# Up projection of a gated FFN: both halves of the moving operand in one matmul, with the low sums copied out and added

## The chip, the cores and the metric

The kernel runs on one core of a Trainium2 chip. The metric is the device time of one execution in microseconds (us): the median of the runs. A core has five engines that run their own instruction streams and meet at semaphores: TensorE (PE in the profile; its weight loads are PEld), VectorE (DVE), ScalarE (ACT), GpSimd (POOL) and SyncE (SP), which here issues the transfers.

## The reference

A small network on 256 tokens of width 1024, batch 1, in float32. Five feed-forward blocks (FFNs) stand in it: four with a causal depthwise convolution of three taps (D_FF 2816), each behind a mixer, and one plain gated block at the end, behind a fifth mixer.

```python
def conv_gated_ffn(xn, w_up, conv_w, conv_b, w_down):
    h = causal_depthwise_conv(xn @ w_up, conv_w, conv_b)
    a, g = jnp.split(h, 2, axis=-1)
    return (jax.nn.silu(g) * a) @ w_down

def swiglu(h, w_gate, w_up, w_down):
    return (jax.nn.silu(h @ w_gate) * (h @ w_up)) @ w_down
```

The mixers (two attentions, a spatial gating, a state space layer, and the last one with a context operand) are untouched.

## The kernel before

**Precision by splitting.** Every large product is made of three: operand and weight are each split into a high part (the value as float32r) and the low rest (what is left of it); `product` (lines 1683, 1684, 1685) adds high x high, weight high x operand low, and weight low x operand high into the same PSUM columns. The operand stands feature-major in XH (highs) and XL (lows), 8 tiles of 128 features by up to 512 columns; the FFNs use the first 256 columns, one per token.

**The weight stream.** Weights come in units of 128 x 2048 floats (1 MB), in the order in which they are used, into a ring of three (raw). For each unit ScalarE copies out the high part (`split_hi`, line 381, writes whi) and VectorE subtracts for the low part (`split_lo`, line 896, writes wlo). whi and wlo are rings of three too: ScalarE waits until TensorE is done with the unit three before (semaphore w_used), and TensorE waits for w_lo before it starts a unit. So the splits run at most three units ahead.

**An FFN** has 33 units: 22 up units (one per tile of 128 value features and 128 gate features) and 11 down units (one per two up units). An up unit j is 2 halves (m) x 8 feature tiles x 3 products of 256 columns = 48 products; its sums, 2 x 256 columns, fill one PSUM bank, 4 or 5 by turns. A down unit has 48 products as well and adds into banks 0 to 3, which hold the whole output and are zeroed ahead with a matmul of zeros. TensorE's order is up 0, up 1, then in a loop (up, up, down) ten times, then the last down. TensorE waits for pp_taken of unit j-2 before it writes a bank again.

**After an up unit** of a conv FFN, VectorE's `take` (line 1068) reads the bank, multiplies it with the row of token scales RSTD, and writes UA in SBUF; ScalarE makes the middle tap and bias of both halves (line 486, waits for pp_taken), VectorE adds two taps each (line 1082, four instructions), ScalarE applies silu to the gate half (line 489), VectorE multiplies (line 1089, writes HID). After two such units ScalarE copies the high part of the hidden pair into HH (line 502) and VectorE subtracts for HL (line 1102), the down unit's operand. HH has one buffer: it waits for the down unit before. In the plain FFN there is no take: silu (line 492) and the multiply (line 1096) read the bank.

**The order is written out by hand**, one program per engine, each strictly in order. A loop iteration (nine in a conv FFN on ScalarE and VectorE, with a head and a tail around them) is, for both up units: ScalarE `split_hi`, taps, silu; VectorE take, `split_lo`, taps, multiply; then a third `split_hi` and HH, a third `split_lo` and HL. The split that stands in the iteration belongs to a later unit: the first to the down unit, the other two to the next two up units.

**Scales.** The first two up units of a conv FFN run while the token scales are still being made; `scale_sums` puts small matmuls among their products, and their results into bank 6. In the fourth FFN the operand of the context is made between iterations (`context_high`, line 411, and `context_operand`, line 1035, called every second iteration as `aside`). In the second FFN GpSimd computes tables for the state space layer beside it.

Of the kernel before, what the change touches and what calls it, by code (L numbers as in the profile page):

```python
# [23 lines left out]
P = 128  # L24
# [102 lines left out]
def program(nc, wst, mst, crow, vec, cst, xin, sgw, sgb, sbc, ctxin, ropes, out):  # L127
    with ExitStack() as ctx:
# [9 lines left out]
        XH = sb("XH", [P, KT, 2 * T], R32)  # L138
        XL = sb("XL", [P, KT, 2 * T], R32)
# [40 lines left out]
        SQ = ar(2048, KT, T)  # L180

# [45 lines left out]
        def s5(i):  # L227
# [58 lines left out]
                 "c_in", "c_row", "ctx_rms", "ctx_inv", "ctx_diag", "ctx_row", "ml_in0", "ml_in1", "ml_used",  # L286
# [84 lines left out]
        def _(act):  # L371
# [67 lines left out]
            def scales():  # L439
# [3 lines left out]
                act.activation(RMSC, PS[:, 6, 0:2], ACT.Sqrt, bias=vcol("eps", 0), scale=1.0 / D)\  # L443
# [29 lines left out]
            def ffn(layer, conv=True, aside=None, tail=None, then=None):  # L473
                u0, q0, up0, hid0 = t.u, t.pp, t.up, t.hid

                def up(j, it=None):
# [3 lines left out]
                    if conv:  # L480
                        act.wait_ge(S["pp_taken"], q0 + j + 1 + 2 * k)
# [8 lines left out]
                    else:  # L490
                        act.wait_ge(S["w_used"], u + 1 + 3 * k)
                        act.activation(SG[:, j % 2, :], PS[:, 4 + (q0 + j) % 2, T:2 * T], ACT.Silu)\
                            .then_inc(S["silu_ready"], 1)

                def hidden(h, it=None):
                    k = 0 if it is None else it

                    act.wait_ge(S["hid_ready"] if conv else S["pp_taken"], (up0 if conv else q0) + 2 * h + 2 + 2 * k)
                    if h > 0:

                        act.wait_ge(S["w_used"], u0 + 2 + 3 * h + 3 * k)
                    act.activation(HH[:, :, :], HID, ACT.Copy).then_inc(S["hh_ready"], 1)

                if conv:
                    scales()
# [382 lines left out]
        def _(dve):  # L888
# [54 lines left out]
            def scales():  # L943
# [12 lines left out]
                dve.tensor_copy(RSTD, PS[:, 6, T:2 * T]).then_inc(S["rstd_row"], 1)  # L956
# [71 lines left out]
            def context_operand(p):  # L1028

                if p == 0:  # L1030
                    dve.wait_ge(S["ctx_in"], 32)
                    dve.wait_ge(S["ctx_row"], 1)
                    link(dve.tensor_copy(RSTX, PS[:, 6, 0:T]))
# [26 lines left out]
            def ffn(layer, conv=True, aside=None, then=None):  # L1060
                u0, q0, up0, hid0 = t.u, t.pp, t.up, t.hid

                def take(j, it=None):
                    k = 0 if it is None else it
                    u = u0 + 2 + 3 * (j // 2 - 1) + j % 2 if j >= 2 else u0 + j
                    bank = PS[:, 4 + (q0 + j) % 2, :].rearrange("p (a b) -> p a b", a=2)
                    dve.wait_ge(S["w_used"], u + 1 + 3 * k)
                    dve.tensor_tensor(UA[:, j % 2], bank, RSTD.unsqueeze(1).broadcast_to([P, 2, T]), ALU.mult)\  # L1068
                        .then_inc(S["pp_taken"], 1)

                def up(j, it=None):
                    k = 0 if it is None else it
                    bank = PS[:, 4 + (q0 + j) % 2, :].rearrange("p (a b) -> p a b", a=2)
                    if conv:

                        dve.wait_ge(S["conv0"], up0 + j + 1 + 2 * k)
                        for back in (1, 2):
# [10 lines left out]
                        dve.wait_ge(S["silu_ready"], up0 + j + 1 + 2 * k)  # L1088
                        dve.tensor_tensor(HID[:, j % 2, :], CA[:, j % 2, 0, :], SG[:, j % 2, :], ALU.mult)\
                            .then_inc(S["hid_ready"], 1)  # L1090
                    else:
                        if j >= 2 and j % 2 == 0:

                            dve.wait_ge(S["hl_ready"], hid0 + j // 2 + k)
                        dve.wait_ge(S["silu_ready"], up0 + j + 1 + 2 * k)
                        dve.tensor_tensor(HID[:, j % 2, :], bank[:, 0, :], SG[:, j % 2, :], ALU.mult)\
                            .then_inc(S["pp_taken"], 1)
# [7 lines left out]
                if conv:  # L1105
                    scales()
                for j in range(2):
                    if conv:
                        take(j)
# [5 lines left out]
                for p, (b, e) in enumerate(parts(n - 1, aside)):  # L1115
                    if aside:
                        aside(p)
                    with dve.Fori(0, e - b) as it:
                        for j in range(2):
                            if conv:  # L1120
                                take(2 + 2 * b + j, it)
# [6 lines left out]
                for j in range(2):  # L1128
                    if conv:
                        take(2 * n + j)  # L1130
# [546 lines left out]
        def _(pe):  # L1677
# [75 lines left out]
            def scale_sums(unit, m, k):  # L1753

                if (unit, m, k) == (0, 1, 3):
                    pe.wait_ge(S["square_sum"], t.free + 1)
                    for c in range(2):
                        for i in range(2):
                            mm = pe.matmul(PS[:, 6, c:c + 1], SQ[:, i, c * P:(c + 1) * P], ones[:, 0:1],
# [757 lines left out]
```

## Time and profile before

| | |
|---|---|
| median of 3 runs | 1827.54 us (1827.36 to 1828.07) |
| the profiled execution, its time | 1829.06 us |
| its span, first to last instruction | 1827.2 us |
| TensorE matmuls busy | 1708.1 us, 93% |
| TensorE weight loads busy (beside the matmuls) | 1616.3 us, 88% |
| VectorE busy | 1248.8 us, 68% |
| ScalarE busy | 844.6 us, 46% |
| GpSimd busy | 163.0 us, 9% |
| mean granted TensorE clock | 0.976 of full |

The profile is of one execution. Busy shares are averages over stages with different limits. A matmul's recorded duration includes its way through the array, so two in a row overlap in the records; what paces TensorE is the distance from start to start. Idle time is put down to the semaphore event that came last.

### The profile page before, as it was taken

How to read it: one execution, taken by the hardware profiler on the slowest of the kernel's cores; microseconds unless marked ns; L12 is line 12 of the kernel's file. 1: busy time of each engine (PE TensorE's matmuls, PEld its weight loads, DVE VectorE, ACT ScalarE, POOL GpSimd, SP SyncE). 2: the span in 40 equal slices, each digit the busy share in tenths (PEclk: the TensorE clock that was granted, in tenths of full speed). 3: DMA queues.
4: the chain of work that ended last, by engine and by line, in shares of the span. 5: the costliest groups of instructions: out<-in, count | busy, mean ns of one | idle time of the engine just before them, and what ended most of it. 6: DMA issues, size and time to landing. Idle time of an engine off the chain costs nothing.

```text
span 1827.2 us, 34733 instructions
## 1 busy us (share of the span) xinstructions
PE 1708.1 (93%) x14503; PEld 1616.3 (88%) x14514; DVE 1248.8 (68%) x1580; ACT 844.6 (46%) x962; POOL 163.0 (9%) x130
## 2 busy tenths in 40 slices
PE   6999999889899997799999999999979899999997
PEld 6979999889899985699999988999978579889997
DVE  5847777786877759767777774777774575664444
ACT  5355554546455530355545445555554533143333
POOL 1002000104910062200000101000000000000000
PEclk9999999999999999999999999999989999899999
DMA  7904545544455423444555761454432121035551
GB/s 299 333 1 162 190 178 184 184 162 152 150 181 184 164 91 117 163 162 162 182 184 181 270 252 47 179 191 168 183 111 93 69 93 70 24 138 184 184 184 69
DMA packets 40050, 286.50 MB, mean 157 GB/s; under 512 B 4576, under 2 KB 4576, under 8 KB 5664
## 3 DMA queue, kind: packets, MB, share of 16 engines
q1 hardware_dynamic: 39024, 280.99, 42.8%
q10 hardware_dynamic: 944, 4.33, 0.7%
q8 instruction: 63, 1.03, 0.2%
q14 instruction: 19, 0.16, 0.0%
HBM read 284.25 MB, written 1.05 MB: 156 GB/s over the span
## 4 chain that ended last, share of the span: by engine, by line
PE 64%; DVE 17%; ACT 9%; issue 6%; POOL 2%; DMA 1%; DVEq 0%; ACTq 0%; POOLq 0%; SPq 0%
PE PS L1683 19%; PE PS L1684 18%; PE PS L1685 18%; ACT whi L381 4%; DVE wlo L896 4%; DVE AR L1082 4%; ACT AR L486 1%; POOL AR L2389 1%; PE PS L1779 1%; DVE AR L1193 1%; DVE XL L940 1%; DVE AR L1190 1%; ACT AR L576 1%; ACT AR L578 1%; PE PS L2235 1%
## 5 line engine op out<-in xcount | busy, mean ns | idle before, releaser
L1683 PE MATMUL PS<-XH,whi 128*128 128x256 f32 (+1 forms) x2696 | 788.8, 293 | 45.0 <-DVE wlo L896 23.8
L1684 PE MATMUL PS<-XL,whi 128*128 128x256 f32 (+1 forms) x2696 | 780.2, 289 | 0.0
L1685 PE MATMUL PS<-XH,wlo 128*128 128x256 f32 (+1 forms) x2696 | 780.1, 289 | 0.0
L896 DVE TENSOR_TENSOR wlo<-raw,whi 128x2048 fp32r<-128x2048 f32 x240 | 558.9, 2331 | 187.7 <-ACT whi L381 187.6
L1683 PEld LDWEIGHTS PS<-XH,whi 128*128 128x128 f32 x2696 | 523.6, 194 | 58.1 <-issue 34.0
L1684 PEld LDWEIGHTS PS<-XL,whi 128*128 128x128 f32 x2696 | 524.1, 194 | 4.4 <-issue 0.2
L1685 PEld LDWEIGHTS PS<-XH,wlo 128*128 128x128 f32 x2696 | 523.7, 194 | 4.1
L381 ACT ACTIVATE whi<-raw 128x2048 fp32r<-128x2048 f32 x240 | 456.0, 1902 | 72.8 <-PE PS L1685 48.4
L1683 PE MATMUL PS<-HH,whi 128*128 128x256 f32 x880 | 251.8, 286 | 13.0 <-DVE HL L1102 8.5
L1685 PE MATMUL PS<-HH,wlo 128*128 128x256 f32 x880 | 251.0, 285 | 0.0
L1684 PE MATMUL PS<-HL,whi 128*128 128x256 f32 x880 | 250.8, 285 | 0.0
L1683 PEld LDWEIGHTS PS<-HH,whi 128*128 128x128 f32 x880 | 170.7, 194 | 14.8 <-DVE HL L1102 9.5
L1082 DVE SCALAR_TENSOR_TENSOR AR<-AR,VEC 128x255 f32<-128x255 f32 (+1 forms) x352 | 161.7, 501 | 15.4 <-ACT AR L486 4.7
L1684 PEld LDWEIGHTS PS<-HL,whi 128*128 128x128 f32 x880 | 170.6, 194 | 0.0
L1685 PEld LDWEIGHTS PS<-HH,wlo 128*128 128x128 f32 x880 | 170.5, 194 | 0.0
L489 ACT ACTIVATE AR<-AR 128x256 f32<-128x256 f32 x88 | 36.7, 418 | 268.4 <-DVE AR L1082 268.4
L2389 POOL TENSOR_TENSOR AR<-AR 128x512 f32<-128x512 f32 x24 | 56.0, 2335 | 916.3 <-ACT AR L435 916.2
L486 ACT ACTIVATE AR<-AR,VEC 128x256 f32<-128x256 f32 x176 | 95.6, 590 | 86.1 <-DVE AR L1068 86.1
L1068 DVE TENSOR_TENSOR AR<-PS,SM 128x512 f32<-128x512 f32 x88 | 60.7, 689 | 27.2 <-PE PS L1685 24.1
L1683 PE MATMUL PS<-whi,XH 128*128 128x256 f32 x256 | 74.1, 289 | 2.5 <-DVE XL L940 2.5
L1684 PE MATMUL PS<-wlo,XH 128*128 128x256 f32 x256 | 73.3, 286 | 0.0
L1685 PE MATMUL PS<-whi,XL 128*128 128x256 f32 x256 | 73.2, 286 | 0.0
(336 smaller groups left out, 1583.7 us busy)
## 6 DMA issues: line engine op xcount, KB each, us to landing
raw<-wst SPq DMA_DIRECT2D x248, 1024.0 KB, 4.8
AR<-mst SPq DMA_DIRECT2D x17, 1024.0 KB, 6.2
XT<-x_in SPq DMA_DIRECT2D x2, 512.0 KB, 6.0
AR<-crow ACTq DMA_DIRECT2D x2, 512.0 KB, 5.8
AR<-sbc ACTq DMA_DIRECT2D x1, 1024.0 KB, 6.6
AR<-ctxin ACTq DMA_DIRECT2D x1, 1024.0 KB, 5.8
y_out<-XT SPq DMA_DIRECT2D x1, 1024.0 KB, 3.9
AR<-sgw ACTq DMA_DIRECT2D x1, 512.0 KB, 3.7
```

The lines of the kernel that those rows point to most:

```text
L381: act.activation(whi[:, r, :], raw[:, u % RING, :], ACT.Copy).then_inc(S["w_hi"], 1)
L486: a = act.activation(CA[:, j % 2, i, :], UA[:, j % 2, i, :], ACT.Identity, bias=cb, scale=w2)
L489: act.activation(SG[:, j % 2, :], CA[:, j % 2, 1, :], ACT.Silu).then_inc(S["silu_ready"], 1)
L576: act.activation(EX[:, p % 2, :], ZC[:, p % 2, :], ACT.Exp).then_inc(S["ex_ready"], 1)
L578: act.activation(LN[:, p % 2, :], EX[:, p % 2, :], ACT.Ln, bias=1.0)\
L896: dve.tensor_tensor(wlo[:, r, :], raw[:, u % RING, :], whi[:, r, :].bitcast(F32), ALU.subtract)\
L1068: dve.tensor_tensor(UA[:, j % 2], bank, RSTD.unsqueeze(1).broadcast_to([P, 2, T]), ALU.mult)\
L1082: ins = dve.scalar_tensor_tensor(y, UA[:, j % 2, i, 0:T - back], w, y, ALU.mult, ALU.add)
L1683: pe.matmul(dst, sh, mh, start=first, stop=False, **kw)
L1684: pe.matmul(dst, sh, ml, start=False, stop=False, **kw)
L1685: return pe.matmul(dst, sl, mh, start=False, stop=last, **kw)
L2389: ins = pool.tensor_tensor(SQ[:, 0:2, :], SQ[:, 0:2, :], SQ[:, 2 * mp:2 * mp + 2, :], ALU.add)
```

## The change

Only the up units of the FFNs change.

TensorE: XH and XL become two views of one tensor XX, so that for a feature tile the 256 highs and the 256 lows of the operand can be read as one moving operand of 512 columns. A group of three products becomes two: weight high x (highs, lows), 512 columns, into a whole bank; and weight low x highs, 256 columns, into the bank's first half. The two halves m take two banks, so unit j takes the pair 4, 5 or the pair 6, 7 by turns. The bank's second half then holds the sums over the lows, which must be added to the first.

ScalarE: a new `lows(j)`, in the program just ahead of the taps of unit j (behind the high split of that half iteration), waits for the unit's products and copies the second halves of both banks (512 columns in all) to LS in SBUF. VectorE: `take` waits for that copy and adds PSUM's first halves and LS into UA; in conv FFNs a second instruction multiplies UA with RSTD. In the plain FFN silu and the multiply read UA instead of the bank.

Banks 6 and 7 being in use, the scale sums of an FFN go to bank 3, and the zeroing of bank 3 moves behind up 1 and waits for their readers.

```diff
-        XH = sb("XH", [P, KT, 2 * T], R32)
-        XL = sb("XL", [P, KT, 2 * T], R32)
+        XX = sb("XX", [P, KT, 4 * T], R32)
+        XH, XL = XX[:, :, 0:2 * T], XX[:, :, 2 * T:4 * T]
...
+        LS = ar(2048, 2, 2, T)
...
+                def lows(j, u, k):
+
+                    b = 4 + 2 * ((q0 + j) % 2)
+                    act.wait_ge(S["w_used"], u + 1 + 3 * k)
+                    act.activation(LS[:, j % 2], PS[:, b:b + 2, T:2 * T], ACT.Copy).then_inc(S["lo_out"], 1)
+
                 def up(j, it=None):
...
                     if conv:
+                        lows(j, u, k)
                         act.wait_ge(S["pp_taken"], q0 + j + 1 + 2 * k)
...
-                        act.wait_ge(S["w_used"], u + 1 + 3 * k)
-                        act.activation(SG[:, j % 2, :], PS[:, 4 + (q0 + j) % 2, T:2 * T], ACT.Silu)\
-                            .then_inc(S["silu_ready"], 1)
+                        lows(j, u, k)
+                        act.wait_ge(S["pp_taken"], q0 + j + 1 + 2 * k)
+                        act.activation(SG[:, j % 2, :], UA[:, j % 2, 1, :], ACT.Silu).then_inc(S["silu_ready"], 1)
...
-                    bank = PS[:, 4 + (q0 + j) % 2, :].rearrange("p (a b) -> p a b", a=2)
-                    dve.wait_ge(S["w_used"], u + 1 + 3 * k)
-                    dve.tensor_tensor(UA[:, j % 2], bank, RSTD.unsqueeze(1).broadcast_to([P, 2, T]), ALU.mult)\
-                        .then_inc(S["pp_taken"], 1)
+                    b = 4 + 2 * ((q0 + j) % 2)
+                    dve.wait_ge(S["lo_out"], up0 + j + 1 + 2 * k)
+                    ins = dve.tensor_tensor(UA[:, j % 2], PS[:, b:b + 2, 0:T], LS[:, j % 2], ALU.add)
+                    if conv:
+                        ins.then_inc(S["up_sum"], 1)
+                        dve.wait_ge(S["up_sum"], up0 + j + 1 + 2 * k)
+                        ins = dve.tensor_tensor(UA[:, j % 2], UA[:, j % 2], RSTD.unsqueeze(1).broadcast_to([P, 2, T]), ALU.mult)
+                    ins.then_inc(S["pp_taken"], 1)
...
-                            mm = product(PS[:, 4 + (q0 + j) % 2, m * T:(m + 1) * T],
-                                         w(slot, kt * 256 + m * P, kt * 256 + m * P + P),
-                                         x(kt), kt == 0, kt == KT - 1)
+                            high, low = w(slot, kt * 256 + m * P, kt * 256 + m * P + P)
+                            both = XX[:, kt, :].rearrange("p (h s t) -> p h s t", h=2, s=2)[:, :, 0, :]
+                            pe.matmul(PS[:, b + m, :].rearrange("p (h t) -> p h t", h=2), high, both, start=(kt == 0), stop=False)
+                            mm = pe.matmul(PS[:, b + m, 0:T], low, XH[:, kt, 0:T], start=False, stop=(kt == KT - 1))
...
-                for b in range(4):
+                def zero(b):
                     pe.matmul(PS[:, b, :], ZB[:, 0:P], ZB[:, :], start=True, stop=False, skip_group_check=True)
+                for b in range(3):
+                    zero(b)
                 up(0)
                 up(1)
+                if free:
+                    pe.wait_ge(S["rstd_row"], t.free)
+                    if t.free == 8:
+                        pe.wait_ge(S["ctx_taken"], 1)
+                zero(3)
```

ScalarE, from the start of a loop iteration of the first FFN to the second high split in it, before (AR are UA, the taps' sums and silu's result by turns; REGISTER_ALU and ISA rows compute loop addresses):

```order
L380 ISA [waits w_loaded2]
L381 ACTIVATE whi<-raw 128x2048 [waits w_used]
L481 ISA
L486 ISA [waits pp_taken]
L486 ACTIVATE AR<-AR,VEC 128x256
L486 ISA
L486 ACTIVATE AR<-AR,VEC 128x256
L488 REGISTER_ALU
L489 ACTIVATE AR<-AR 128x256 [waits conv2]
L378 REGISTER_ALU
L380 REGISTER_ALU [waits w_loaded0]
L381 ACTIVATE whi<-raw 128x2048 [waits w_used]
```

and after:

```order
L382 ACTIVATE whi<-raw 128x2048 [waits w_used]
L480 REGISTER_ALU
L481 ACTIVATE AR<-PS 128x512 [waits w_used]
L489 ISA
L494 ISA [waits pp_taken]
L494 ACTIVATE AR<-AR,VEC 128x256
L494 ISA
L494 ACTIVATE AR<-AR,VEC 128x256
L496 REGISTER_ALU
L497 ACTIVATE AR<-AR 128x256 [waits conv2]
L379 REGISTER_ALU
L382 ACTIVATE whi<-raw 128x2048 [waits w_used,w_loaded0]
```

The copy L481, which waits for the unit's products, now stands between the high split and the taps; the taps' wait is behind it.

VectorE, the same iteration, from the multiply that makes the first HID to the second low split, before:

```order
L1089 TENSOR_TENSOR AR<-AR 128x256 [waits silu_ready]
L1067 REGISTER_ALU
L1068 TENSOR_TENSOR AR<-PS,SM 128x512 [waits w_used]
L895 REGISTER_ALU
L896 TENSOR_TENSOR wlo<-raw,whi 128x2048 [waits w_hi]
```

and after:

```order
L1104 TENSOR_TENSOR AR<-AR 128x256 [waits silu_ready]
L1076 REGISTER_ALU
L1077 TENSOR_TENSOR AR<-PS,AR 128x512 [waits lo_out]
L1081 TENSOR_TENSOR AR<-AR,SM 128x512 [waits up_sum]
L903 REGISTER_ALU
L904 TENSOR_TENSOR wlo<-raw,whi 128x2048 [waits w_hi]
```

The take L1068 has become the add L1077, which waits for ScalarE's copy, and the multiply L1081, which waits for the add; the low split stands behind both.

TensorE, the start of its loop of the first FFN, before:

```order
L1797 ISA [waits pp_taken]
L1683 MATMUL PS<-XH,whi 128x256 [waits w_lo]
L1684 MATMUL PS<-XL,whi 128x256
L1685 MATMUL PS<-XH,wlo 128x256
L1683 MATMUL PS<-XH,whi 128x256
L1684 MATMUL PS<-XL,whi 128x256
L1685 MATMUL PS<-XH,wlo 128x256
```

and after:

```order
L1801 ISA [waits pp_taken]
L1809 MATMUL PS<-XX,whi 128x512 [waits w_lo]
L1810 MATMUL PS<-XX,wlo 128x256
L1809 MATMUL PS<-XX,whi 128x512
L1810 MATMUL PS<-XX,wlo 128x256
L1809 MATMUL PS<-XX,whi 128x512
L1810 MATMUL PS<-XX,wlo 128x256
```

Three products of 256 columns have become one of 512 and one of 256, and the unit's waits are those of before.

## Rows read from the trace of the kernel before

**Rows 1.** Timeline, VectorE, first FFN, HL alone: start, us, engine, line
```profile
171.30 0.69 DVE L1102 TENSOR_TENSOR HL<-AR,HH 128x512 fp32r<-128x512 f32 x1 [0.70 <-ACT HH L502]
...
238.68 0.69 DVE L1102 TENSOR_TENSOR HL<-AR,HH 128x512 fp32r<-128x512 f32 x1
...
255.95 0.69 DVE L1102 TENSOR_TENSOR HL<-AR,HH 128x512 fp32r<-128x512 f32 x1
...
339.25 0.69 DVE L1102 TENSOR_TENSOR HL<-AR,HH 128x512 fp32r<-128x512 f32 x1 [0.69 <-ACT HH L502]
```

**Rows 2.** Timeline, VectorE, first FFN, second loop iteration
```profile
188.09 0.69 DVE L1102 TENSOR_TENSOR HL<-AR,HH 128x512 fp32r<-128x512 f32 x1
188.69 0.69 DVE L1068 TENSOR_TENSOR AR<-PS,SM 128x512 f32<-128x512 f32 x1
189.29 2.28 DVE L896 TENSOR_TENSOR wlo<-raw,whi 128x2048 fp32r<-128x2048 f32 x1
191.49 1.90 DVE L1082 SCALAR_TENSOR_TENSOR AR<-AR,VEC 128x255 f32<-128x255 f32 x4
193.88 0.42 DVE L1089 TENSOR_TENSOR AR<-AR 128x256 f32<-128x256 f32 x1 [0.48 <-ACT AR L489]
...
195.68 2.29 DVE L896 TENSOR_TENSOR wlo<-raw,whi 128x2048 fp32r<-128x2048 f32 x1 [0.70 <-ACT whi L381]
...
204.28 0.68 DVE L1102 TENSOR_TENSOR HL<-AR,HH 128x512 fp32r<-128x512 f32 x1
```

**Rows 3.** Timeline, ScalarE, the same iteration
```profile
193.42 0.42 ACT L489 ACTIVATE AR<-AR 128x256 f32<-128x256 f32 x1 [2.77 <-DVE AR L1082]
193.75 1.90 ACT L381 ACTIVATE whi<-raw 128x2048 fp32r<-128x2048 f32 x1
...
200.14 1.90 ACT L381 ACTIVATE whi<-raw 128x2048 fp32r<-128x2048 f32 x1
201.94 0.61 ACT L502 ACTIVATE HH<-AR 128x512 fp32r<-128x512 f32 x1
202.46 1.90 ACT L381 ACTIVATE whi<-raw 128x2048 fp32r<-128x2048 f32 x1
```

**Rows 4.** Timeline, VectorE, first and last HL, second and fourth FFN
```profile
456.78 1.90 DVE L1102 TENSOR_TENSOR HL<-AR,HH 128x512 fp32r<-128x512 f32 x1 [0.70 <-ACT HH L502]
...
633.38 0.69 DVE L1102 TENSOR_TENSOR HL<-AR,HH 128x512 fp32r<-128x512 f32 x1 [0.69 <-ACT HH L502]
...
1164.83 0.69 DVE L1102 TENSOR_TENSOR HL<-AR,HH 128x512 fp32r<-128x512 f32 x1 [0.70 <-ACT HH L502]
...
1336.92 0.69 DVE L1102 TENSOR_TENSOR HL<-AR,HH 128x512 fp32r<-128x512 f32 x1 [0.69 <-ACT HH L502]
```

**Rows 5.** Timeline, TensorE, last mixer, 512-column products
```profile
1370.52 0.39 PE L1683 MATMUL PS<-XH,whi 128*128 128x512 f32 x1
...
1371.20 0.39 PE L1683 MATMUL PS<-XH,whi 128*128 128x512 f32 x1
```

**Rows 6.** Groups by line and shape: count, busy us, mean ns, idle before
```profile
L719 ACT ACTIVATE AR<-PS 128x512 f32<-128x512 f32 x8 | 4.3, 596 | 21.4 <-PE PS L1685 21.4
```

**Rows 7.** Timeline, VectorE then ScalarE, fourth FFN, between two iterations
```profile
1200.40 0.69 DVE L1102 TENSOR_TENSOR HL<-AR,HH 128x512 fp32r<-128x512 f32 x1
...
1201.52 0.91 ACT L411 ACTIVATE XH<-AR,MODV 128x256 fp32r<-128x256 f32 x2 [2.84 <-DVE AR L1035]
1202.33 1.90 ACT L381 ACTIVATE whi<-raw 128x2048 fp32r<-128x2048 f32 x1
```

**Rows 8.** Timeline, TensorE, two waits (in brackets the wait, its releaser)
```profile
340.00 0.39 PE L1683 MATMUL PS<-HH,whi 128*128 128x256 f32 x1 [1.75 <-DVE HL L1102]
...
495.93 0.54 PE L1683 MATMUL PS<-XH,whi 128*128 128x256 f32 x1 [3.36 <-DVE wlo L896]
```

**Rows 9.** Windows behind these waits: stretch, us, PE busy, PEclk, DMA
```profile
340.10:343.50 3.40, 3.40 (x29) 1.00 0.04 14
496.00:499.40 3.40, 3.40 (x16) 0.50 0.63 219
```

More of the change, by code:

```diff
@@ L490, in up @@
                     else:
[L491 to L493 removed]
+                        lows(j, u, k)
+                        act.wait_ge(S["pp_taken"], q0 + j + 1 + 2 * k)
+                        act.activation(SG[:, j % 2, :], UA[:, j % 2, 1, :], ACT.Silu).then_inc(S["silu_ready"], 1)
                 def hidden(h, it=None):
                     k = 0 if it is None else it
[L498 removed]
+                    act.wait_ge(S["hid_ready"], up0 + 2 * h + 2 + 2 * k)
                     if h > 0:
@@ L504, in ffn @@
                 if conv:
-                    scales()
+                    scales(3)
                 act.preload_act_table(ACT.Silu)
@@ L1087, in up @@
                                 ins.then_inc(S["conv2"], 1)
[L1088 to L1097, printed above, removed]
+                    if j >= 2 and j % 2 == 0 and not conv:
+                        dve.wait_ge(S["hl_ready"], hid0 + j // 2 + k)
+                    dve.wait_ge(S["silu_ready"], up0 + j + 1 + 2 * k)
+                    value = CA[:, j % 2, 0, :] if conv else UA[:, j % 2, 0, :]
+                    dve.tensor_tensor(HID[:, j % 2, :], value, SG[:, j % 2, :], ALU.mult).then_inc(S["hid_ready"], 1)
                 def hidden(h, it=None):
@@ L1105, in ffn @@
                 if conv:
-                    scales()
+                    scales(3)
                 for j in range(2):
-                    if conv:
-                        take(j)
+                    take(j)
                     ahead(u0 + j)
@@ L1119, in ffn @@
                         for j in range(2):
-                            if conv:
-                                take(2 + 2 * b + j, it)
+                            take(2 + 2 * b + j, it)
                             split_lo(s1 + 3 * b + j, it)
@@ L1128, in ffn @@
                 for j in range(2):
-                    if conv:
-                        take(2 * n + j)
+                    take(2 * n + j)
                     split_lo(s1 + j)
@@ L1751, in tokens, with scale_sums @@
                 t.u += 1
-            def scale_sums(unit, m, k):
+            def scale_sums(unit, m, k, bank=6):
                 if (unit, m, k) == (0, 1, 3):
@@ L1771, in scale_sums @@
                     for c in range(2):
-                        mm = pe.matmul(PS[:, 6, c * P:(c + 1) * P], ones, DG[:, c * P:(c + 1) * P], start=True, stop=True)
+                        mm = pe.matmul(PS[:, bank, c * P:(c + 1) * P], ones, DG[:, c * P:(c + 1) * P], start=True, stop=True)
                     mm.then_inc(S["ctx_row"], 1)
```

21 lines of the change are left out of this document (11 added, 10 removed).

## The prediction

> **What bounds the kernel now.** Read the by-engine part of the page first: TensorE is busy nearly all the time, so the question is what paces it in the five feed-forward blocks (FFNs), the only part that changes. The start times of one VectorE instruction that occurs once per loop iteration, the subtraction that makes HL, answer it. In the first FFN's steady part two of them stand 17.27 us apart [rows 1], and an iteration holds 3 weight units of 48 products: 17.28 / 144 = 0.120 us a product. TensorE is the bound, at its own pace.
>
> Then the timeline of VectorE and ScalarE in an iteration where TensorE happened to be ahead. There HL follows HL after 204.28 - 188.09 = 16.19 us [rows 2], with no wait for TensorE in it. These two engines pass work to each other in program order, and the chain closes on itself. Read from start to start: HL to take 0.60; take to split 0.60; split to taps 2.20; taps to silu 1.93; silu to the next high split 0.33; that to its low split 1.93; split to taps 2.20; taps to silu 1.93; silu to high split 0.33; to low split 1.93; to HL 2.21 [rows 2, 3]. The sum is 16.19. So this loop is only 1.1 us shorter than TensorE's 17.28; that is all the slack there is, and shares of busy time do not show it.
>
> The same instruction in the second and the fourth FFN (first to last of 11) spans 176.60 and 172.09 us, against 339.25 - 171.30 = 167.95 in the first (the third repeats the first) [rows 1, 4]. In these two the VectorE loop already bounds part of the time: GpSimd work stretches VectorE instructions in the second, and preparation of the context operand stands between iterations in the fourth.
>
> **The change, part by part.**
>
> *TensorE.* A group of three products of 256 columns costs 0.360 us. It becomes one of 512 and one of 256. The trace has 512-column products of the same operands in the last mixer: three take 0.68 us, 0.227 each [rows 5]. A group becomes 0.227 + 0.120 = 0.347, 0.013 less; a unit of 16 groups 0.213 less; an iteration with two up units 16.85 us instead of 17.28. If TensorE bounded everywhere, 110 up units would give 23.4 us. The Trainium skill (TensorE: Matmul & The Clock Gate, Back-to-back issue gap) gives a spacing of N/2.4 + 2.5 ns; by it a group would fall from 328 to 325 ns, which would leave only some 4 us of the 23.4. The rows are above that formula by 11 ns at either width, so a fixed cost is paid per product, and I use the rows.
>
> *The copy (ScalarE).* A Copy of 128x512 out of two banks takes 0.596 us [rows 6], with a hand-over of 0.04 (silu 193.42 + 0.42 to the multiply at 193.88 [rows 2, 3]) 0.64. In each half of an iteration it stands behind a high split, 1.80 after that split's start (201.94 - 200.14); what follows HH starts 0.52 after it [rows 3].
>
> *The add and the multiply (VectorE).* Before, one instruction of 0.69 out of PSUM, the take, with 0.60 to the next [rows 2]. Now an add of the same shape, a hand-over to itself (0.69 + 0.04 = 0.73), and the multiply, which I price as the same instruction.
>
> *What this does to the loop.* Odd unit: before, its low split began 0.33 + 1.93 = 2.26 us after the even unit's silu, with take long done. Now ScalarE must finish the high split before it copies: 0.33 + 1.80 + 0.64 (copy) + 0.73 (add) + 0.60 (multiply) = 4.10. That is 1.84 more. Even unit: HL start to low split was 1.20; now ScalarE runs HH, a high split and the copy (from HL's predecessor 1.80 + 0.52 + 1.80 + 0.64 = 4.76 after a high split's start, against 4.14 for HL), so the add begins 0.62 after HL, then 0.73 + 0.60: 1.95, 0.75 more. The loop becomes 16.19 + 1.84 + 0.75 = 18.78 us. TensorE at 16.85 now waits 1.9 us in every iteration.
>
> *A conv FFN.* Up to the first HL: 0.73 + 1.84 = 2.6 later. First iteration: HH to the copy's end is 0.52 + 1.80 + 0.64, less 0.65 to HL (HH's 0.61 and a hand-over), so the add comes 2.31 after HL instead of 0.62: 18.78 + 1.69 = 20.47. Eight at 18.78: 150.24. Last (no third split, so HL follows silu by 0.46 + 0.47 + 0.65 instead of 4.47): 15.89. Together 186.6 against 167.95, +18.6; with the start +21.2. First and third FFN: 42.4.
> Second: 176.60 before. The stretching by GpSimd (8.65 over the first FFN visible, more than that hidden by slack) adds about 10 in full: 196.6, so +20.0 + 2.6 = 22.6.
> Fourth: at each of four places the context operand puts two VectorE and two ScalarE steps ahead of the next high split. From HL to the end of the two ScalarE steps is 1202.33 - 1200.40 = 1.93, and HL to the add becomes 1.93 + 1.80 + 0.64 = 4.37 [rows 7] instead of 0.62, 3.75 more, three times; the first time 2.5 (it replaces 2.31, and has a copy of 0.46 more); the fifth about 0.8. 186.6 + 14.6 = 201.2 against 172.09: +29.1 + 2.6 = 31.7.
> The last FFN has no taps and no multiply; its engines have room, so it keeps TensorE's pace: 22 x 0.213 = -4.7. Its end is set by HH waiting for the product unit ahead, which does not change.
> Sum: 42.4 + 22.6 + 31.7 - 4.7 = +92.0.
>
> *The clock.* TensorE now waits longer, most of all ahead of each conv FFN's last down unit: HL starts 15.89 after the one before, while TensorE is done after 0.11 + 5.55 + 5.76 = 11.4, so with HL's own 0.7 it idles 5.2 us, where it idled 1.75 [rows 8]. After a wait of 1.75 the granted clock stayed 1.00 (2.4 GHz); after one of 3.36 it was 0.50 (1.2 GHz) for 3.4 us [rows 8, 9], which costs 1.7. Four times 1.7 is 6.8, on the path. The GpSimd stretch gets two more such waits, about 1.2 net. Elsewhere in the loop waits are about 1 us each. I add 8.
>
> Total: +100. The profiled execution took 1829.06 us (span 1827.2); 1929, or 1927.5 from the median of 1827.54. I say 1927.
>
> **The bounds.** Copy: from nothing on the path (then the two adds alone remain, 1.46 a loop, 17.65; the whole sum some 31 lower) to 0.73; I take the Copy row, the same form. Add and multiply: from 0.60 to 0.80 each. Cheap ends of both together lower the sum by some 20, dear ends raise it by 14; the clock from 0 to 16. Hence 1903 to 1949.
>
> **The rivals.**
> *TensorE stays the bound.* Then -23.4: 1829.1 - 23.4 = 1806, the other side. It needs the ScalarE-VectorE loop to stay below 16.85, thus to grow by less than 0.66 instead of 2.59. For it: both engines are busy only 68% and 46%. Against it: the 16.19 with nothing waiting for TensorE. Even with the copy free the two extra adds exceed 0.66. 4%.
> *The copy hides.* If sums end early enough and ScalarE slips the copy into a wait, only the adds lengthen the loop: 17.65, total +61 + 8: about 1897. Against it: ScalarE's order puts a 1.9 us split right ahead of each odd copy. 8%.
> *The clock falls in every iteration.* With 1.9 us of wait in 18.8, in two pieces of 0.8 and 1.0, a fall of 3.4 us per iteration would cost 1.7, of which 0.54 is slack before an even copy: 36 x 1.16 = 42 more, 1969. For it: a fall follows every long wait. Against: 1.75 in one piece brought none [rows 8, 9]. 7%.
> *The edit does nothing measurable*, gain and loss cancelling: the loop would have to be 17.3 to 17.4. 1%.
> The forecast itself has 80%.
>
> **How the numbers follow.** 1927 is the likeliest case; its own range, 1903 to 1949, holds nearly all of its 80%, so it is the range. No change can be told within 0.2%, about 3.7 us; the copy-hides and clock cases are slower too, so faster 4%, same 1%, slower 95%.
>
> **What will show it.** HL to HL in the first FFN near 18.8 us, not 16.9. Idle time ahead of the add should be put down to ScalarE's copy, and TensorE's idle time to the low split, twice an iteration. The product of 512 columns should be spaced 0.227 and the pair 0.347, visible in the last FFN, where HL stands 16.85 apart. Clock 0.50 at each conv FFN's end. Wrong would be: a copy much longer than 0.6, a pair slower than 0.36 (which in the conv FFNs would still be hidden), or a loop other than 18.8.

## The result

The changed kernel takes 1927.78 us (median of 4 runs, 1924.5 to 1932.19) against 1827.45 for the one before: the ratio is 1.0551, 95% interval 1.0535 to 1.0568. It is slower by 100 us; forecast were 1927, a range of 1903 to 1949, and 95% for slower.

The page of the changed kernel's profiled execution: the span, busy time by engine, and three groups of section 5 (count, busy us, mean ns, then idle time before and what ended it).

```profile
span 1923.6 us, 31472 instructions
## 1 busy us (share of the span) xinstructions
PE 1726.9 (90%) x12754; PEld 1533.7 (80%) x12754; DVE 1315.7 (68%) x1690; ACT 907.3 (47%) x1072; POOL 160.5 (8%) x130
...
L1809 PE MATMUL PS<-XX,whi 128*128 128x512 f32 x1760 | 640.9, 406 | 57.3 <-DVE wlo L904 53.9
L904 DVE TENSOR_TENSOR wlo<-raw,whi 128x2048 fp32r<-128x2048 f32 x240 | 559.0, 2332 | 115.1 <-ACT whi L382 115.0
...
L1077 DVE TENSOR_TENSOR AR<-PS,AR 128x512 f32<-128x512 f32 x110 | 75.8, 689 | 176.2 <-ACT AR L481 176.1
```

VectorE's add now idles 176.2 us ahead, 176.1 of it ended by ScalarE's copy (L481); before, the take idled 27.2 us, mostly for TensorE. And TensorE's wide products (L1809) idle 57.3 us ahead, 53.9 of it ended by the low split (L904). The span grew by 1923.6 - 1827.2 = 96.4 us.

The same instruction as in [rows 1], HL on VectorE, first FFN of the changed kernel (start, duration, line):

```profile
174.50 0.69 DVE L1109 TENSOR_TENSOR HL<-AR,HH 128x512 fp32r<-128x512 f32 x1 [0.70 <-ACT HH L510]
...
194.92 0.69 DVE L1109 TENSOR_TENSOR HL<-AR,HH 128x512 fp32r<-128x512 f32 x1
...
213.65 0.68 DVE L1109 TENSOR_TENSOR HL<-AR,HH 128x512 fp32r<-128x512 f32 x1
...
344.72 0.68 DVE L1109 TENSOR_TENSOR HL<-AR,HH 128x512 fp32r<-128x512 f32 x1
...
360.33 0.69 DVE L1109 TENSOR_TENSOR HL<-AR,HH 128x512 fp32r<-128x512 f32 x1 [0.70 <-ACT HH L510]
```

The iterations are 18.7 us long (213.65 - 194.92 = 18.73), where they were 16.2 to 17.3; the first is 20.42 and the last 15.61. The forecast was 18.78, 20.47 and 15.89. From the first HL to the last it is 185.83 us against 167.95 [rows 1].

One iteration of it, VectorE, the counterpart of [rows 2]:

```profile
232.37 0.69 DVE L1109 TENSOR_TENSOR HL<-AR,HH 128x512 fp32r<-128x512 f32 x1
232.97 0.68 DVE L1077 TENSOR_TENSOR AR<-PS,AR 128x512 f32<-128x512 f32 x1
233.69 0.69 DVE L1081 TENSOR_TENSOR AR<-AR,SM 128x512 f32<-128x512 f32 x1
234.30 2.29 DVE L904 TENSOR_TENSOR wlo<-raw,whi 128x2048 fp32r<-128x2048 f32 x1
236.50 1.89 DVE L1094 SCALAR_TENSOR_TENSOR AR<-AR,VEC 128x255 f32<-128x255 f32 x4
238.88 0.43 DVE L1104 TENSOR_TENSOR AR<-AR 128x256 f32<-128x256 f32 x1 [0.48 <-ACT AR L497]
241.17 0.69 DVE L1077 TENSOR_TENSOR AR<-PS,AR 128x512 f32<-128x512 f32 x1 [1.86 <-ACT AR L481]
241.89 0.69 DVE L1081 TENSOR_TENSOR AR<-AR,SM 128x512 f32<-128x512 f32 x1
242.50 2.28 DVE L904 TENSOR_TENSOR wlo<-raw,whi 128x2048 fp32r<-128x2048 f32 x1
...
251.09 0.68 DVE L1109 TENSOR_TENSOR HL<-AR,HH 128x512 fp32r<-128x512 f32 x1
```

And ScalarE, the counterpart of [rows 3]:

```profile
238.43 0.42 ACT L497 ACTIVATE AR<-AR 128x256 f32<-128x256 f32 x1 [2.77 <-DVE AR L1094]
238.75 1.90 ACT L382 ACTIVATE whi<-raw 128x2048 fp32r<-128x2048 f32 x1
240.56 0.58 ACT L481 ACTIVATE AR<-PS 128x512 f32<-128x512 f32 x1
...
248.76 0.61 ACT L510 ACTIVATE HH<-AR 128x512 fp32r<-128x512 f32 x1
249.28 1.90 ACT L382 ACTIVATE whi<-raw 128x2048 fp32r<-128x2048 f32 x1
251.08 0.57 ACT L481 ACTIVATE AR<-PS 128x512 f32<-128x512 f32 x1
```

VectorE ends the even unit's multiply at 238.88 + 0.43 and stands until 241.17. Meanwhile ScalarE, behind silu, runs the 1.9 us high split from 238.75, then the copy (240.56), and only the copy's end at 241.14 lets the add go. Silu 238.43 to low split 242.50 is 4.07 us (forecast 4.10, before 2.26). At the end of the iteration HL at 251.09 is followed by the add after 0.60 and the low split 1.33 after that (234.30 - 232.97): 1.93 in all, forecast 1.95.

The five FFNs, from first to last HL, in us; the rows of before are [rows 1, 4]:

| FFN | before | after | grew | forecast of the growth |
|---|---|---|---|---|
| first | 167.95 | 185.83 | 17.9 | 18.6 |
| second (GpSimd beside it) | 176.60 | 196.26 | 19.7 | 20.0 |
| third | 167.95 | 185.85 | 17.9 | 18.6 |
| fourth (context operand) | 172.09 | 204.75 | 32.7 | 29.1 |
| plain | 171.98 | 166.84 | -5.1 | -4.7 with its start |

What is left, 13.4 us, lies between the blocks: each block's first HL comes 2.3 to 3.2 us later after what precedes it. For the four conv FFNs these sum to 10.65 us, for the plain one it is 2.8.

The plain FFN's row must not be read as its gain. Its first and last HL, before and then after:

```profile
1635.19 0.69 DVE L1102 TENSOR_TENSOR HL<-AR,HH 128x512 fp32r<-128x512 f32 x1 [0.70 <-ACT HH L502]
...
1807.17 0.69 DVE L1102 TENSOR_TENSOR HL<-AR,HH 128x512 fp32r<-128x512 f32 x1 [5.64 <-ACT HH L502]
```

```profile
1736.72 0.69 DVE L1109 TENSOR_TENSOR HL<-AR,HH 128x512 fp32r<-128x512 f32 x1 [0.70 <-ACT HH L510]
...
1903.56 0.69 DVE L1109 TENSOR_TENSOR HL<-AR,HH 128x512 fp32r<-128x512 f32 x1 [2.61 <-ACT HH L510]
```

The first HL comes later and the iteration behind it is shorter by about as much (13.19 us against 16.40), so most of the -5.1 only makes up for the late start. From the fourth FFN's last HL to the plain one's last it is 470.25 us before (1807.17 - 1336.92) and 467.89 after (1903.56 - 1435.67): 2.4 less, half of the forecast 4.7, which counted the start too.

**One wait that was not forecast.** HL of the fourth FFN of the changed kernel, first, second and last:

```profile
1230.92 0.69 DVE L1109 TENSOR_TENSOR HL<-AR,HH 128x512 fp32r<-128x512 f32 x1 [0.69 <-ACT HH L510]
...
1258.43 0.69 DVE L1109 TENSOR_TENSOR HL<-AR,HH 128x512 fp32r<-128x512 f32 x1
...
1435.67 0.69 DVE L1109 TENSOR_TENSOR HL<-AR,HH 128x512 fp32r<-128x512 f32 x1 [0.70 <-ACT HH L510]
```

The first iteration is 27.51 us, not 20.47 + 2.5 = 23.0. TensorE's timeline says why (its second row is the wait ahead of the first FFN's last down unit, the counterpart of [rows 8]):

```profile
1232.09 0.58 PE L1837 MATMUL PS<-ZB 128*128 128x512 bf16 x1 [11.50 <-DVE AR L1041]
...
361.08 0.38 PE L1687 MATMUL PS<-HH,whi 128*128 128x256 f32 x1 [4.55 <-DVE HL L1109]
```

The zeroing of bank 3 waited 11.50 us for L1041, VectorE's copy of the context's scale row out of bank 3, which in program order stands behind the first HL.

**The clock.** TensorE's granted clock in two stretches of the changed kernel (us, PE busy, PEclk, DMA share, GB/s), behind the 4.55 us wait at 361.08 and at the place where the next stage starts:

```profile
361.40:364.80 3.40, 3.40 (x19) 0.52 0.02 7
377.20:380.60 3.40, 3.40 (x30) 1.00 0.93 320
```

and in the kernel before, at the start of that next stage:

```profile
356.10:359.50 3.40, 3.40 (x17) 0.50 0.89 320
```

The fall behind the last down unit's wait came as forecast, 0.52 for 3.4 us. But the kernel before has one of its own some 16 us later, which the changed kernel has not: here the fall moved, it was not added. The other three FFN ends are not all alike. Behind the second FFN it moved as well. Behind the third both stand in the changed kernel (0.55 from 1061.60, and again 0.55 from 1078). Behind the fourth the kernel before already has one, after a wait of the same 1.75 us as in [rows 8] (TensorE's row, then the window behind it):

```profile
1337.66 0.39 PE L1683 MATMUL PS<-HH,whi 128*128 128x256 f32 x1 [1.75 <-DVE HL L1102]
...
1338.60:1342.00 3.40, 3.40 (x20) 0.57 0.00 0
```

So of the four falls that were forecast there, one was new. And within the loop there is none: from the second HL of the changed kernel's first FFN to the tenth (194.92 to 344.72) the granted clock is 1.00.

### The profile page after: what moved, and what is told of

Read it like the earlier page. It is cut to its first block, busy times and chain, and to the rows that moved or that the text cites. A ratio compares the mean times of both kernels' runs of the same rounds, so it can differ in the third digit from the quotient of the medians.

```text
span 1923.6 us, 31472 instructions
## 1 busy us (share of the span) xinstructions
PE 1726.9 (90%) x12754; PEld 1533.7 (80%) x12754; DVE 1315.7 (68%) x1690; ACT 907.3 (47%) x1072; POOL 160.5 (8%) x130
## 4 chain that ended last, share of the span: by engine, by line
PE 40%; DVE 29%; ACT 14%; issue 13%; POOL 2%; DVEq 1%; DMA 1%; ACTq 0%; POOLq 0%; SPq 0%
ACT whi L382 9%; DVE wlo L904 8%; PE PS L1687 8%; PE PS L1688 8%; PE PS L1689 8%; DVE AR L1094 7%; PE PS L1809 5%; DVE AR L1077 3%; PE PS L1810 3%; DVE HL L1109 1%; ACT AR L481 1%; DVE AR L1081 1%; POOL AR L2402 1%; PE PS L1783 1%; DVE AR L1197 1%
## 5 line engine op out<-in xcount | busy, mean ns | idle before, releaser
L1809 PE MATMUL PS<-XX,whi 128*128 128x512 f32 x1760 | 640.9, 406 | 57.3 <-DVE wlo L904 53.9
L904 DVE TENSOR_TENSOR wlo<-raw,whi 128x2048 fp32r<-128x2048 f32 x240 | 559.0, 2332 | 115.1 <-ACT whi L382 115.0
L1810 PE MATMUL PS<-XX,wlo 128*128 128x256 f32 x1760 | 495.8, 282 | 0.0
L1809 PEld LDWEIGHTS PS<-XX,whi 128*128 128x128 f32 x1760 | 333.1, 189 | 156.4 <-DVE wlo L904 73.7
L1810 PEld LDWEIGHTS PS<-XX,wlo 128*128 128x128 f32 x1760 | 335.4, 191 | 0.2
L1687 PE MATMUL PS<-XX,whi 128*128 128x256 f32 (+1 forms) x936 | 283.3, 303 | 29.7 <-DVE wlo L904 15.4
L1687 PE MATMUL PS<-HH,whi 128*128 128x256 f32 x880 | 257.9, 293 | 38.2 <-DVE HL L1109 19.8
L1688 PE MATMUL PS<-XX,whi 128*128 128x256 f32 (+1 forms) x936 | 278.7, 298 | 0.0
L1689 PE MATMUL PS<-XX,wlo 128*128 128x256 f32 (+1 forms) x936 | 278.5, 297 | 0.0
L1687 PEld LDWEIGHTS PS<-XX,whi 128*128 128x128 f32 x936 | 183.3, 196 | 37.9 <-issue 30.7
L1077 DVE TENSOR_TENSOR AR<-PS,AR 128x512 f32<-128x512 f32 x110 | 75.8, 689 | 176.2 <-ACT AR L481 176.1
L1688 PEld LDWEIGHTS PS<-XX,whi 128*128 128x128 f32 x936 | 183.3, 196 | 4.4 <-issue 0.2
L1689 PEld LDWEIGHTS PS<-XX,wlo 128*128 128x128 f32 x936 | 182.9, 195 | 4.2
L1688 PEld LDWEIGHTS PS<-HL,whi 128*128 128x128 f32 x880 | 176.1, 200 | 0.0
L1689 PEld LDWEIGHTS PS<-HH,wlo 128*128 128x128 f32 x880 | 176.0, 200 | 0.0
L494 ACT ACTIVATE AR<-AR,VEC 128x256 f32<-128x256 f32 x176 | 96.4, 595 | 149.7 <-DVE AR L1081 149.7
```

Source lines behind the costliest of these rows:

```text
L494: a = act.activation(CA[:, j % 2, i, :], UA[:, j % 2, i, :], ACT.Identity, bias=cb, scale=w2)
L904: dve.tensor_tensor(wlo[:, r, :], raw[:, u % RING, :], whi[:, r, :].bitcast(F32), ALU.subtract)\
L1077: ins = dve.tensor_tensor(UA[:, j % 2], PS[:, b:b + 2, 0:T], LS[:, j % 2], ALU.add)
L1687: pe.matmul(dst, sh, mh, start=first, stop=False, **kw)
L1688: pe.matmul(dst, sh, ml, start=False, stop=False, **kw)
L1689: return pe.matmul(dst, sl, mh, start=False, stop=last, **kw)
```

## The experiments

The theory is the prediction's: ScalarE and VectorE form a closed loop in each conv iteration (taps, silu, splits, take), the copy and the add lengthen it by 1.84 + 0.75 us, and it overtakes TensorE. Its rival: the time comes from TensorE itself, from how the wide and narrow products run, or from its clock behind longer waits. Every ratio is to the kernel before, on the same chip. Differences from the changed kernel's 1927.78 us may be between chips, on which the kernel before took 1827.45 to 1828.08 us.

**products_only.** The changed products without the copy and the add; the sums over the operand's lows are left out. In the plain FFN, where VectorE had the add, it copies the first halves out instead.

```diff
-                        lows(j, u, k)
-                    dve.wait_ge(S["lo_out"], up0 + j + 1 + 2 * k)
-                    ins = dve.tensor_tensor(UA[:, j % 2], PS[:, b:b + 2, 0:T], LS[:, j % 2], ALU.add)
+                    dve.wait_ge(S["w_used"], u + 1 + 3 * k)
+                    ins = dve.tensor_tensor(UA[:, j % 2], PS[:, b:b + 2, 0:T], ..., ALU.mult)
```

> The changed products with neither the copy nor the add: VectorE's take multiplies the banks' first halves with the scales right away, as before the change. Left out of the computation: the sums over the operand's lows. Theory 1 (the ScalarE-VectorE chain bounds the changed kernel): that chain is back at 16.2 us an iteration, TensorE bounds again, now at 16.85, so HL to HL is 16.85 and the time falls below that of before, to about 1813 (conv FFNs -10, plain FFN -5). Theory 2 (the 512-column product itself, or its two-piece operand, is slow in the FFNs): HL to HL stays well above 17.28 and the time stays near the changed kernel's 1928. Theory 3 (the clock): falls of the granted clock remain without long waits.

1825.77 us, ratio 0.9987 (0.9978 to 0.9997). The loops are back under TensorE, so copy and add are what slowed the changed kernel; the rival, by which TensorE itself did, is out. But HL to HL is 17.07, not 16.85, and the bank 3 wait is there too (8.97 us of TensorE, first iteration of the fourth FFN 25.4 us against 19.32): two misses that together leave 2 us of the expected 15. The wait alone takes back 6.1; at 17.07 the products save 0.21 us an iteration where 0.43 was reckoned, half as much.

**three_products.** The changed kernel with three products a group. The sums over the highs and over the lows of the operand are interleaved in one bank, which changes what is summed; only its time is read.

```diff
-                            pe.matmul(PS[:, b + m, :]..., high, both, start=(kt == 0), stop=False)
+                            pe.matmul(PS[:, b + m, 0:T], high, XH[:, kt, 0:T], start=(kt == 0), stop=False)
+                            pe.matmul(PS[:, b + m, T:2 * T], high, XL[:, kt, 0:T], start=(kt == 0), stop=(kt == KT - 1), ...)
```

> The changed kernel with its copy, add and banks, but TensorE's group is three products of 256 columns again (weight high x highs into the first half, weight high x lows into the second, weight low x highs into the first). Theory 1: in the conv FFNs nothing changes, HL to HL stays at 18.73, since TensorE's 17.28 still fits; in the plain FFN it goes from 16.85 to 17.28, so about +5: 1932. Theory 2: without the 512-column product the time falls to near 1828.

1928.28 us, ratio 1.0552 (1.0535 to 1.057): the changed kernel's, where 1932 was expected. HL to HL stays 18.73 in the conv FFNs and goes from 17.07 to 17.28 in the plain one (first to last 169.19 against 166.84, so 2.4 us and not 5). In the conv FFNs the whole TensorE part of the change is invisible.

**no_mult.** The changed kernel without the multiply by the scales in the conv FFNs, which is left out of the computation.

```diff
-                    if conv:
-                        ins.then_inc(S["up_sum"], 1)
-                        dve.wait_ge(S["up_sum"], up0 + j + 1 + 2 * k)
-                        ins = dve.tensor_tensor(UA[:, j % 2], UA[:, j % 2], ..., ALU.mult)
```

> The changed kernel without the second VectorE instruction of the take in the conv FFNs. Left out of the computation: the scaling of the up sums by the token scales. Theory 1: the multiply is in the chain twice an iteration at about 0.73 each, so HL to HL goes from 18.73 to about 17.3 and the time falls by about 60, to 1866. Rival (only ScalarE's copy and what it waits for set the pace, VectorE's second instruction hides behind ScalarE): HL to HL stays within 0.3 of 18.7 and the time within 10 of 1928.

1862.56 us, ratio 1.02 (1.0183 to 1.0217), 65 less. Two HLs of its first FFN:

```profile
226.08 0.68 DVE L1105 TENSOR_TENSOR HL<-AR,HH 128x512 fp32r<-128x512 f32 x1
...
243.35 0.68 DVE L1105 TENSOR_TENSOR HL<-AR,HH 128x512 fp32r<-128x512 f32 x1
```

17.27 apart: the multiply was twice in the chain, at 0.73.

**copy_first.** The changed kernel with the copy ahead of the high split (`copied` is the wait and copy that stood in `up`).

```diff
                         for j in range(2):
+                            copied(2 + 2 * b + j, it)
                             split_hi(s1 + 3 * b + j, it)
-                            up(2 + 2 * b + j, it)
+                            up(2 + 2 * b + j, it)
```

> The changed kernel with one thing moved in the conv FFNs: ScalarE's copy of the low sums stands ahead of the high split of its half iteration, not behind it. Theory 1 (1.84 of the chain's growth in the odd unit is the copy waiting behind the split): the low split now begins 2.8 us after silu instead of 4.1, HL to HL falls from 18.73 to about 17.5 and the time by about 62, to 1866. Rival (the copy waits for TensorE, not for the split): less than 10 of it.

1869.19 us, ratio 1.0231 (1.0214 to 1.0248), 59 less. VectorE in its first FFN:

```profile
250.36 0.43 DVE L1115 TENSOR_TENSOR AR<-AR 128x256 f32<-128x256 f32 x1 [0.48 <-ACT AR L501]
250.84 0.69 DVE L1088 TENSOR_TENSOR AR<-PS,AR 128x512 f32<-128x512 f32 x1
251.57 0.69 DVE L1092 TENSOR_TENSOR AR<-AR,SM 128x512 f32<-128x512 f32 x1
252.65 2.29 DVE L915 TENSOR_TENSOR wlo<-raw,whi 128x2048 fp32r<-128x2048 f32 x1 [0.38 <-ACT whi L382]
```

The low split starts 2.74 us after silu (249.91), no longer 4.07. The last row shows one thing more: add and multiply are over at 252.26 (251.57 + 0.69), and the low split then waits 0.38 us for the high split. With the copy out of its way, the second VectorE instruction costs the odd unit nothing. The mean of HL to HL is about 17.7, a little above 17.5, since ScalarE now waits for TensorE before its split in the even unit.

**ctx_early.** The changed kernel with the context row copied earlier.

```diff
                     up(j)
+                    if aside and j == 0:
+                        dve.wait_ge(S["ctx_row"], 1)
+                        dve.tensor_copy(RSTX, PS[:, 3, 0:T]).then_inc(S["ctx_taken"], 1)
```

> The changed kernel, with the copy of the context's scale row out of bank 3 moved on VectorE from behind the first HL of the fourth FFN to behind its first up unit. Theory 1a (the zeroing of bank 3 waits for this copy and holds up TensorE by 11.5 us, which makes the first iteration 27.5 us instead of the forecast 22.9): the wait goes, the first iteration comes to about 23 and the total falls by 4 to 6, to 1923. Rival (TensorE's wait there is covered by the chain of the other two engines anyway): no change within 1 us.

1920.16 us, ratio 1.0508 (1.049 to 1.0525), 7.6 less by the medians and 6.2 in the profiled spans, a little more than the expected 4 to 6. The first iteration of the fourth FFN is 22.47 (27.51 - 22.47 = 5.0) and TensorE's wait at the zeroing 2.02 instead of 11.50.

**base_mid.** The kernel before with the high splits of the conv FFNs between taps and silu (`between` calls `split_hi`). HH now stands ahead of the third split.

```diff
                         a.then_inc(S["conv0"], 1)
+                        between()
                         act.wait_ge(S["conv2"], up0 + j + 1 + 2 * k)
...
-                            split_hi(s1 + 3 * b + j, it)
-                            up(2 + 2 * b + j, it)
-                        split_hi(s1 + 3 * b + 2, it)
-                        hidden(1 + b, it)
+                            up(2 + 2 * b + j, it, lambda: split_hi(s1 + 3 * b + j, it))
+                        hidden(1 + b, it)
+                        split_hi(s1 + 3 * b + 2, it)
```

> The kernel before the change, with one thing moved in the conv FFNs: ScalarE's high splits stand between the taps and silu of a unit (where it waits for VectorE's taps anyway), one split earlier than before. Theory 1 (a closed chain of the two engines, with the split behind silu in it) says that both 1.93 us pieces from split to split leave the chain, so it drops from 16.2 to about 14.9 us and TensorE alone bounds: HL to HL 17.28 everywhere, the fourth FFN's pairs of iterations 34.6 instead of 35.05, and heads and the second FFN gain; in all -18: 1810. Rival (the chain has nothing to do with the split's place; the engines just follow TensorE): within 3 us of 1828.

1811.99 us, ratio 0.9917 (0.9901 to 0.9934). ScalarE in a first-FFN iteration, taps, split, silu:

```profile
245.13 1.09 ACT L486 ACTIVATE AR<-AR,VEC 128x256 f32<-128x256 f32 x2 [1.47 <-DVE AR L1091]
246.14 1.90 ACT L381 ACTIVATE whi<-raw 128x2048 fp32r<-128x2048 f32 x1
249.00 0.42 ACT L491 ACTIVATE AR<-AR 128x256 f32<-128x256 f32 x1 [0.97 <-DVE AR L1105]
```

The split at 246.14 ends at 248.04 and silu, which waits for VectorE's taps, starts at 249.00: the split costs the chain nothing. And VectorE's take and HL of that iteration:

```profile
238.51 0.69 DVE L1091 TENSOR_TENSOR AR<-PS,SM 128x512 f32<-128x512 f32 x1 [3.10 <-PE PS L1708]
...
252.00 0.69 DVE L1125 TENSOR_TENSOR HL<-AR,HH 128x512 fp32r<-128x512 f32 x1
```

The take had to wait 3.10 us for TensorE, where it waited about 1 in the kernel before. HL to HL is 17.28 and in the first iteration, where TensorE does not bound, 14.45. The fourth FFN's pairs of iterations fell from 35.05 to 34.56.

The gain does not come from the first FFN's steady part, which stays at 17.28. From first to last HL the second FFN takes 3.3 us less, the fourth 5.0, the first and the third 1.2 each, and the conv FFNs' first HLs come 5.3 us earlier in all. The remaining 3.0 of the profiled execution's 19.0 us (the median fell by 16.1) lie ahead of the plain FFN's first HL, where the order is as before, and may be scatter.

**after_mid_ctx.** The changed kernel with both moves (base_mid's and ctx_early's).

> The changed kernel with the same move of the high splits, and with the early copy of the context's scale row. Theory 1: the chain falls from 18.73 to about 15.5, TensorE bounds at 17.07, and the time is about that of before: conv FFNs +3, plain FFN -5: 1826. Rival (copy and add cost what they cost, wherever the splits stand): the time stays above 1880.

1833.46 us, ratio 1.0032 (1.0021 to 1.0044). HL to HL is 17.07, so TensorE bounds again with copy and add in place; but it is 7 us above the expected 1826. The first iteration is 17.15 us (14.45 in base_mid) and TensorE waits 3.22 ahead of each last down unit (1.75 before the change): in head and tail nothing seems to cover copy and add. The kernel to compare it with is base_mid, on the same chip: against its 1811.99 us this is 21.5 more. So where TensorE bounds the steady part the change still costs, in the second FFN (first to last HL 181.08 against 173.27) and ahead of the conv FFNs' first HLs, each 1.9 to 3.2 us later. With 1833.46 the change is a loss in this order of the program too.

**plain_mid.** base_mid, and the change in the plain FFN alone (its diff is base_mid's, and that of the change for the plain FFN alone).

> The kernel before with the moved high splits, and the change (512-column operand, copy, add) in the plain FFN alone. Theory 1: -18 from the moved splits and -4.5 from the plain FFN: 1805, faster than both kernels. Rival (the plain FFN's gain is eaten by its longer end chain or by the clock): the same as the kernel with the moved splits alone.

1809.36 us, ratio 0.9895 (0.9879 to 0.9912); a second series, **plain_mid_again**, gave 1809.09, ratio 0.9898 (0.9881 to 0.9914).

> The kernel before with the moved high splits and the changed plain FFN, products by turns, as the one to compare with on the same chip: HL to HL 17.07 in the plain FFN, 1809 to 1810.

Both are about 1% faster than the kernel before, but 4 us above the expected 1805. That they are faster than base_mid by 2.6 is inside the scatter of the two medians, so the rival is not excluded. The traces show the plain FFN's first HL to last at 166.62 against 171.98, but again with a later first HL: from the fourth FFN's last HL to the plain one's last it is 466.99 and 466.47 against base_mid's 467.28. Whether the change pays in the plain FFN alone is open.

**one_piece.** The changed kernel, with the plain FFN's wide operand contiguous.

```diff
+                                pe.matmul(PS[:, b + m, :], high, XX[:, kt, 0:2 * T], start=(kt == 0), stop=False)
```

> The changed kernel, where the plain FFN's 512-column operand is one contiguous piece instead of two of 256 columns a kilobyte apart. Left out there: the lows of the operand are replaced by other columns of the same tensor. Theory A (the gap between the pieces costs the 7 ns by which the pair stands above 0.347): HL to HL in the plain FFN falls from 17.07 to 16.85 and the time by 2.3. Theory B (the extra time comes from a wide and a narrow product alternating, not from the gap): HL to HL stays 17.07, no change.

1924.51 us, ratio 1.0525 (1.0508 to 1.0543); HL to HL in the plain FFN stays 17.07. The gap between the pieces costs nothing. The median's 3 us below the changed kernel's are no more than its scatter: its profiled span is 1926.6.

**wide_first.** plain_mid with a half unit's eight wide products ahead of its eight narrow ones.

```diff
-                        for kt in range(KT):
-                            (wide, narrow)
+                        for kt in range(KT):
+                            (wide)
+                        for kt in range(KT):
+                            (narrow)
```

> The kernel before with the moved high splits and the changed plain FFN, where TensorE runs a half unit's eight 512-column products first and its eight 256-column products behind them, instead of by turns. If the 7 ns above 0.347 a pair come from the alternation of widths, a unit falls by 0.11 us and HL to HL in the plain FFN from 17.07 to 16.85, the time by 2.3 against the same kernel with products by turns. If each wide product of the FFN costs 0.234 by itself, HL to HL stays 17.07.

1809.88 us, ratio 0.9906 (0.9889 to 0.9923), the same as by turns (1809.09 on this chip). TensorE in its plain FFN (groups of eight):

```profile
1700.41 2.00 PE L1833 MATMUL PS<-XX,whi 128*128 128x512 f32 x8
1702.25 1.12 PE L1836 MATMUL PS<-XX,wlo 128*128 128x256 f32 x8
1703.20 2.00 PE L1833 MATMUL PS<-XX,whi 128*128 128x512 f32 x8
```

Eight wide take 1.84, eight narrow 0.95, so 0.349 a pair against 0.353; HL to HL goes from 17.07 to 16.93. The turns between widths explain 0.14 of the 0.21 us an iteration.

## Why the prediction was right, and where it was not

*TensorE bounds before, with a loop of 16.19 behind it, 1.1 shorter.* Shown from both sides: with the moved splits the shortest iteration (the last of a block aside) is 14.42 us and no longer 16.18, and where the loop bounded, the time falls to TensorE's pace; the copy and the add push the loop above it.

*The loop's growth by 1.84 and 0.75.* Measured 4.07 - 2.26 = 1.81 and 1.93 - 1.20 = 0.73, loop 18.73. no_mult and copy_first take the multiply and the wait behind the split out of it, and the time falls as it should. This is the step that made the prediction.

*What remains if the copy is free.* Mispriced, in the bounds and in two rivals. The prediction lets the extra VectorE instruction cost 0.73 in each half, a loop of 17.65. But [rows 2] show VectorE idle for 0.70 us ahead of the odd unit's low split, waiting for the high split, and copy_first shows the instruction vanish in this gap. It would have cost the even unit alone: 16.19 + 0.73 = 16.92, below TensorE's measured 17.07. So the hidden copy, had it come, would have left TensorE the bound and, by this estimate, a time near that of before, not 1897. (no_mult saves 0.73 in both halves, since there the copy still ends behind the high split.)

*TensorE's group at 0.347.* Mis-sized. Changed kernel, plain FFN:

```profile
1770.00 0.40 PE L1809 MATMUL PS<-XX,whi 128*128 128x512 f32 x1
1770.23 0.28 PE L1810 MATMUL PS<-XX,wlo 128*128 128x256 f32 x1
1770.35 0.40 PE L1809 MATMUL PS<-XX,whi 128*128 128x512 f32 x1
```

0.35 from pair to pair; over a whole iteration, less a down unit's 48 x 0.120 = 5.76, it is (17.07 - 5.76) / 32 = 0.353. The row of a run of wide products [rows 5] doesn't hold where wide and narrow alternate. By the formula of the Trainium skill (TensorE: Matmul & The Clock Gate, Back-to-back issue gap) a pair would take 0.325, an estimate further off than the rows. In the conv FFNs it cost nothing, since three_products shows that they do not see TensorE's part. In the plain FFN it halved the gain: 22 x 16 x 0.007 = 2.5 us instead of 4.7, and 2.4 were measured.

*The fourth FFN, +29.1.* It grew by 32.7. The diff's `zero(3)` waits for the context row's copy, and the prediction has no term for this wait. The copy stands in VectorE's order behind the first HL; ctx_early puts the wait at 5.0 us of the first iteration. Without it the block would have grown by 27.6, 1.5 less than forecast, half of which is what every conv FFN fell short of its 186.6.

*The clock, +8.* Wrong in its net size. The fall behind each last down unit came, but twice it displaced the one at the next stage's start, and once it had been there before; the rule that 1.75 us brings none was read from one wait, and the fourth FFN's end breaks it. Between the first FFN's last HL and the second's first the trace grew by 119.95 - 117.53 = 2.4, and the four conv FFNs' starts together by 10.65, against 4 x 2.6 = 10.4 forecast for the later HL alone. No time is left for the clock there.

*The range.* By the prediction's own terms the low end is 1927 - 20 - 8 = 1899 and not 1903.

So +92 of work and +8 of clock were forecast, and 96.4 in the spans (and 100.3 in the medians) measured. The clock's 8 and 1.8 in the first three FFNs were too much; the fourth FFN's 3.6 and the plain FFN's 2.3 were too little. These partly cancel. That the median comes within 1 us of the forecast is luck, the more so as the four runs lie between 1924.5 and 1932.19; that it lies far inside the range, and why, is not. The rival of a hidden copy is refuted by VectorE's 176 us behind it, that of TensorE as the bound by products_only and three_products, and that of a clock that falls in every iteration by the 1.00 between 194.92 and 344.72.

## What to carry to other kernels

Before a change hands work from a nearly saturated engine to two that look idle, read an iteration in which the saturated one was ahead: the length of the other engines' closed chain, not their busy share, is the room there is (here 1.1 us of 17.3 with engines 68% and 46% busy). A long independent instruction, such as the split here, belongs in front of a wait that happens anyway and not between two steps of such a chain; moving it gave 16.1 us, and the change at most 55 x 0.21 = 11.6 with the measured pair, an estimate. And compare a change with the best order of the old program, not only with the old program: after_mid_ctx looks level with the one and is 21.5 us behind the other. And a wait that the diff adds must be placed in the program order of the engine that answers it.

## What the runs showed of the hardware

Products of 512 columns follow each other at 0.227 us and of 256 at 0.120, but a pair by turns takes 0.353 and not 0.347; eight and eight take 0.349 a pair. That the wide operand lies in two pieces makes no difference. What the remaining 2 ns are is open.

Of four waits of 1.74 or 1.75 us in the kernel before, each ahead of a conv FFN's last down unit, three left the granted clock at 1.00 and one, the fourth FFN's, was followed by 0.57. The waits of 3.22 us there in after_mid_ctx were followed by 0.50 to 0.52, those of 4.55 to 4.66 in the changed kernel by 0.50 to 0.55. A fall also came without a long wait, at 356.10 in the kernel before, behind waits of 0.40 to 1.27 us with little work between them. And a fall may only replace one that the next waits would have brought: its cost can't be added up wait by wait.
